# The second MLP's up-projection in channel order: high and low weight products one after the other for each tile, instead of in two groups of eight

## The reference, cut to what matters

```python
h = rms_norm(x, g_mlp[l])
x = x + jnp.square(jax.nn.relu(h @ w_mlp_up[l])) @ w_mlp_down[l]   # 2048 -> 8192 -> 2048
```

## Time and profile before

| | us |
|---|---|
| median of 3 runs (2945.84 to 2946.53) | 2945.89 |
| the profiled execution, its own time | 2946.16 |
| its span, from the first to the last instruction | 2944.3 |
| TensorE busy in the span | 2925.5 (99%) |
| TensorE weight loads busy (they overlap the products) | 2421.7 (82%) |
| VectorE busy | 2014.6 (68%) |
| ScalarE busy | 1424.4 (48%) |

### The profile page before, as it was taken

How to read it: one execution, slowest core, us unless ns; L and a number is a source line. 1 busy time by engine, 2 the same in 40 slices (tenths; PEclk the granted TensorE clock), 3 DMA queues, 4 the chain that set the end, 5 groups by cost and what they waited for, 6 DMA issues and landing times.

```text
span 2944.3 us, 44625 instructions
## 1 busy us (share of the span) xinstructions
PE 2925.5 (99%) x15677; PEld 2421.7 (82%) x15677; DVE 2014.6 (68%) x2650; ACT 1424.4 (48%) x1877; POOL 305.5 (10%) x272
## 2 busy tenths in 40 slices
PE   9999999999999999999999999999999999999998
PEld 7888877788888888888888877777888888888887
DVE  6755777656677777768678677777655666666666
ACT  5445656554444444446555553434545444444444
POOL 0002960000000000000000063332000000000000
PEclk9999999999999999999999999999999999999999
DMA  6555453455555565555565533333665555555554
GB/s 234 180 186 168 147 165 130 156 188 189 183 189 186 178 198 181 194 189 181 190 223 181 179 127 124 121 125 135 225 218 194 190 191 191 189 190 192 189 190 156
DMA packets 145454, 525.84 MB, mean 179 GB/s; under 512 B 16128, under 2 KB 16384, under 8 KB 144592
## 3 DMA queue, kind: packets, MB, share of 16 engines
q1 hardware_dynamic: 139840, 505.21, 52.0%
q0 software_dynamic: 1760, 10.55, 1.0%
q10 hardware_dynamic: 3760, 8.78, 0.8%
HBM read 516.09 MB, written 8.39 MB: 178 GB/s over the span
## 4 chain that ended last, share of the span: by engine, by line
PE 95%; DVE 2%; ACT 1%; issue 1%; DMA 1%; ACTq 0%; DVEq 0%; SPq 0%; POOLq 0%; POOL 0%
PE bank L2256 50%; PE bank L2261 25%; PE bank L2908 7%; PE bank L2912 4%; PE bank L2698 1%; PE bank L2360 1%; PE bank L2284 1%; DVE w_lo L1411 1%; PE bank L2439 1%; ACT w_hi L786 0%; PE bank L2505 0%; PE bank L2727 0%; DMA w_raw<-weights 0%; PE bank L2368 0%; PE bank L2454 0%
## 5 line engine op out<-in xcount | busy, mean ns | idle before, releaser
L1411 DVE TENSOR_TENSOR w_lo<-w_raw,w_hi 128x1024 fp32r<-128x1024 f32 x956 | 1187.7, 1251 | 758.3 <-ACT w_hi L786 757.5
L786 ACT CAST w_hi<-w_raw 128x1024 fp32r<-128x1024 f32 x956 | 1005.0, 1052 | 1370.0 <-PE bank L2261 1159.0
L2256 PE MATMUL bank<-w_hi,a_both 128*128 128x512 f32 x4672 | 1185.0, 395 | 3.1 <-DVE a_both L1425 1.6
L2256 PEld LDWEIGHTS bank<-w_hi,a_both 128*128 128x128 f32 x4672 | 864.4, 188 | 190.8 <-issue 11.2
L2261 PE MATMUL bank<-w_lo,a_both 128*128 128x512 f32 x2336 | 630.4, 390 | 1.2 <-DVE w_lo L1411 1.2
L2261 PEld LDWEIGHTS bank<-w_lo,a_both 128*128 128x128 f32 x2336 | 438.6, 188 | 94.6 <-DVE w_lo L1411 1.9
L2908 PE MATMUL bank<-a_both,w_hi 128*128 128x512 f32 x960 | 240.1, 392 | 0.0
L2908 PEld LDWEIGHTS bank<-a_both,w_hi 128*128 128x128 f32 x960 | 173.6, 189 | 31.7
L2256 PE MATMUL bank<-w_hi,m_lo 128*128 128x512 f32 x480 | 186.9, 389 | 0.0
L2256 PE MATMUL bank<-w_hi,m_hi 128*128 128x512 f32 x480 | 186.9, 389 | 0.0
L2912 PEld LDWEIGHTS bank<-a_both,w_lo 128*128 128x128 f32 x960 | 131.0, 190 | 9.4
(11 more groups left out here) (434 smaller groups left out, 2605.0 us busy)
## 6 DMA issues: line engine op xcount, KB each, us to landing
w_raw<-weights SPq DMA_DIRECT2D x952, 512.0 KB, 3.3
gate<-gate_st ACTq DMA_DIRECT2D x8, 512.0 KB, 2.7
h<-gate ACTq DMA_DIRECT2D x8, 512.0 KB, 4.9
gain<-gains POOLq DMA_DIRECT2D x3, 1024.0 KB, 6.5
h<-x_tok SPq DMA_DIRECT2D x4, 512.0 KB, 6.8
w_raw<-w_proj SPq DMA_DIRECT2D x4, 512.0 KB, 4.9
h_rest<-h POOLq DMA_DIRECT2D x1, 2048.0 KB, 8.7
h<-h_rest POOLq DMA_DIRECT2D x1, 2048.0 KB, 9.5
```

The costliest lines, as they stand in the source:

```text
L786: nc.scalar.copy(w_hi[:, s, :], w_raw[:, s, :]).then_inc(hi_ready, 1)
L1411: V.tensor_tensor(w_lo[:, s, :], w_raw[:, s, :], w_hi[:, s, :].bitcast(F32), ALU.subtract).then_inc(lo_ready, 1)
L2256: T.matmul(psum[t][:], left[:, t * P:(t + 1) * P], wh, start=start and j == 0 and n == 0, stop=False)
```

## The change

In `channel_chunk` the two groups of eight products become one loop. For each of the eight weight tiles the wide product with the high part is followed at once by the narrow one with the low part. The wait for the low part moves up, ahead of the slab's first product, beside the wait for the high part. The products are the same, and so is the place of `slab_done`, behind the last narrow one. Within a bank the additions come in another order.

```diff
                     pe.wait_ge(hi_ready, QUAD * u + s + 1)
+                    pe.wait_ge(lo_ready, QUAD * u + s + 1)
                     for k, ct, w in places:
                         T.matmul(bank[4 + ct][:].rearrange("p (b s) -> p b s", b=2), w_hi[:, s, w], a_both[:, :, k],
                                  start=k == 0, stop=False)
-                    pe.wait_ge(lo_ready, QUAD * u + s + 1)
-                    for k, ct, w in places:
                         last = T.matmul(bank[4 + ct][:, 0:SEQ], w_lo[:, s, w], a_hi[:, k], start=False, stop=k == KT - 1)
                     last.then_inc(slab_done, 1)
```

## The result

The changed kernel is slightly slower: 2950.19 us against 2945.98 for the kernel before (medians of 17 runs each), 4.2 us more. The ratio is 1.0016 with a 95% interval of 1.0009 to 1.0022. It is less than the 0.2% that the forecast used as its bound for "the same", but clear of noise, and on the other side of no change than the forecast. The time lies inside the stated range of 2937 to 2952; the direction is wrong.

A forecast was written before the change was run, and what follows sets the result against it. TensorE, 99% busy, was taken to bound the kernel, with no wait to remove; a pair at 0.347 us makes a slab 2.776 instead of 2.793, 2.0 us less over 120 slabs: 2946.16 - 2.0 = 2944.1 us, range 2937 to 2952.

The forecast's parts named there:

- the wait moved up: Wait for the low part, now ahead of the slab's first product: zero cost, as the shortest lead found is 4.35 us.
- Adding to the bank just written: Each narrow product adds to the bank that the wide one before it has just written: taken as zero cost.
- where the weight loads lie: A load behind a narrow product is now followed by one with 0.226 us: gain of nothing to 0.01 us per narrow product.
- the sum: Wide product 0.226 to 0.227 us plus narrow 0.12 gives 0.347 a pair, 2.0 us less for 120 slabs.
- The other sum: The two neighbours at a change of product length, 0.235 + 0.11 us, give 0.345 for a pair.
- Rival (c): Wide products behind narrow ones stay disturbed, narrow ones get no early start: pair 0.36 us, time 2956.5; chance 0.14.
- Rival (a): The order of wide and narrow products makes no difference: pair 0.349 us, time 2945.9; chance 0.26 with near surroundings.
- Rival (b): Weight loads get out of each other's way: pair 0.336 to 0.34 us, time 2933.4 to 2937.3; chance 0.18.
- Rival (d): The wait for the low part becomes the later one: 3093 us at a whole subtraction per slab; chance 0.01.
- The loads' durations: Sign in the profile after: narrow-line loads with a median of 188 ns, against 192, if the pressure on them is gone.
- The rule from the Trainium skill: Loads fit under each product in any order; 109 ns narrow, 216 ns wide, a pair 0.325 us before and after: zero.

The follow-up runs named there:

- runs of two: Two wide, two narrow products in turn in every slab, against the changed kernel's alternation: 2945.38 us, ratio 0.9997; only in each chunk's first slab: 2944.92 us.
- runs of four: Four wide, four narrow products in turn in every slab, against the changed kernel's alternation: 2948.24 us, ratio 1.0007; only in each chunk's first slab: 2945.24 us.

## Why the prediction was wrong

**What held.** The two lines wait for nothing, before or after, and the wait moved up is free: 2946.20 against 2946.30 us with that edit alone. Adding to the bank just written is free. The path is TensorE's alone, so 0.0044 us for each of 960 pairs (4.2 us in the medians) went straight to the end.

**The step that failed** is the one on where the weight loads lie, and with it the sum. It bounded the effect of the new places "between nothing and 0.12 - 0.11 = 0.01 us" of gain for each narrow product and gave no bound above zero; the sum then took a wide product "at the pace without disturbance" and came to 0.347 for a pair. In 14 of 15 chunks a pair takes 0.353. The argument was that behind each pressed load comes one with time to spare. The runs showed that this doesn't settle the pair: in the later chunks the full load of a wide product beside a narrow one goes with 0.353, one of 96 columns with 0.347, one of 64 with 0.340. With the wait and the bank excluded by runs of their own, the whole difference lies in this term, 0.353 for 0.347.

**The sum itself described a pace that exists, by luck.** 0.347 is what the first chunk does behind its transposes, and what the later chunks do when runs of two or four stand ahead of the alternation. But its parts aren't those of the sum. The forecast had the wide product undisturbed at 0.2267 and the narrow one at its steady 0.12; at the fast pace the wide ones hold the engine for 0.230 to 0.233 us and the narrow ones for 0.112 to 0.118. Two errors of some 0.005 us cancel. The other sum that it gave, of the two neighbours at a change of length, 0.235 + 0.11, has the right parts. Above all, the forecast treated the pace as a property of the pair. It is one of the pair and of what ran before it.

**The rivals.** Rival (c), never settled, had the direction and in part the mechanism: at the slow pace the wide products hold the engine for 0.232 to 0.241 us, and of three narrow ones two lose the early start (0.118 and 0.120) and one keeps it (0.113). It had priced a pair at 0.36; measured was 0.353, well under half of the way from 0.349, and below the 0.355 from which it would decide. Rival (a) fell, since the order alone moved a pair from 0.349 to 0.353. Rival (b)'s 0.340 is the pace of this alternation with 64 stationary columns for the wide products; with full loads it was never reached. Rival (d) didn't occur.

**The loads' durations** were to show whether the pressure is gone. Line 2911's median is 189 ns, against 192 before. By the forecast's reading most of the pressure was gone, and yet the pair got slower. That median doesn't measure the pace.

**The rule from the Trainium skill** that the forecast named ("TensorE: Matmul & The Clock Gate", section "Back-to-back issue gap") gave zero, with 109 and 216 ns for the two products. (The section calls this the gap of an isolated product, which the forecast left out.) Held for some products, the best that the runs here show is 113 and 227. The rule has no term for order or entry. The measurements have one: 0.006 us for a pair by the entry, with full loads, and 0.010 by the order, with 64 columns for the wide products (2.80 us for a slab against 2.72).

**What stays open.** Why the same products settle at 0.347 or 0.353, what in an entry decides it, why runs of four are worse than runs of two and of eight, and why the wide run behind short-load narrow products still loses its 0.03 us. The runs show that the pace depends on the stationary columns, on unequal lengths (at equal ones each product takes 0.226 to 0.227 us) and on the entry, and that it isn't the bank, the wait or the number of changes. A mechanism inside TensorE wasn't isolated.

## What to carry to other kernels

On a saturated TensorE the order of long and short products with full stationary operands is worth a few thousandths of a microsecond for each, either way; read it from the distances of starts over several periods, and don't add up single products' best values. If a sequence repeats in a loop, look at each place where it is entered: the same code may run at two paces, and a few products of another order ahead of it can choose the better one. Which order does so has to be measured at each entry: here runs of two ahead of the alternation gave the fast pace directly, and the slow one where eight transposes stood between. And compare a variant with both paces of the original before a gain is put down to what was changed.

## What the hardware showed that was not expected

- One alternating sequence has two stable paces, 0.347 and 0.353 us for a pair, each kept over at least 56 pairs, to the end of the chunk. The slow one repeats every three pairs (1.06 us). Differences of a few nanoseconds behind the same eight transposes go with one or the other.
- With 64 stationary columns for the wide products the sequence settled at 0.340 us from both entries, by the chunk's second slab where products of 512 columns stood ahead.
- Less loading can be slower: 64 stationary columns for the wide products in groups of eight gave 2.80 us for a slab in 14 of 15 chunks, and full ones 2.793. In the first chunk they gave 2.787.
